# Filler products left out of the routing, and the last experts' combines issued one expert later

## The reference

```python
for layer in range(DEPTH):                       # DEPTH = 2
    hn = rms_norm(h, attn_norm_g[layer])
    mix = mixer_ab(...) if layer % 2 == 0 else mixer_c(...)
    h = h + mix
    h = h + hierarchical_moe(rms_norm(h, ffn_norm_g[layer]), ...)
return rms_norm(h, final_norm_g)

# hierarchical_moe: softmax over 4 groups, best group; top 2 of its 8 experts
# 32 experts in all; each: h = silu(xb @ w_gate[e]) * (xb @ w_up[e]);  y = h @ w_down[e]
# w_gate, w_up: 1024 x 512, w_down: 512 x 1024, all float32; y is added back with the gate's weight
```

## Time and profile before

| | |
|---|---|
| median of three runs | 1139.12 us |
| the profiled execution | 1137.95 us |
| its span, first to last instruction | 1136.1 us |
| mean granted clock of TensorE | 0.877 of full speed |
| TensorE matmul busy | 830.9 us (73%) |
| VectorE, ScalarE, GpSimd busy | 162.2, 153.8, 67.7 us |
| moved by DMA | 438.33 MB, mean 386 GB/s |
| chain that ended last | DMA 50%, PE 40%, issue 6% |

### The profile page before, as it was taken

The page is one execution under the profiler, slowest core; times in us unless marked ns, Lnnn a source line. Parts: engine busy times, 40 slices in busy tenths (PEclk is TensorE's granted clock), DMA queues, the critical chain, the costliest instruction groups (busy, mean ns, idle before and its releaser), DMA issues.

```text
span 1136.1 us, 13784 instructions
## 1 busy us (share of the span) xinstructions
PE 830.9 (73%) x5942; PEld 440.3 (39%) x5942; DVE 162.2 (14%) x438; ACT 153.8 (14%) x343; POOL 67.7 (6%) x88
## 2 busy tenths in 40 slices
PE   9999999835666474738789999955657464746876
PEld 7685684311313131314444576321313122211624
DVE  1143442000000000000014535100000000000002
ACT  2246231000000000000010444100000000000101
POOL 0010020000000000000001552000000000000000
PEclk9999999977878697868989999986878778877988
DMA  9942669999999999999999648999999999999994
GB/s 376 421 185 112 267 277 379 427 446 439 425 423 441 430 430 425 448 427 427 427 417 425 237 177 322 427 428 446 432 424 423 444 439 418 427 449 427 429 426 181
DMA packets 22544, 438.33 MB, mean 386 GB/s; under 512 B 2528, under 2 KB 3552, under 8 KB 7008
## 3 DMA queue, kind: packets, MB, share of 16 engines
q1 hardware_dynamic: 21232, 434.39, 90.2%
q10 hardware_dynamic: 1264, 3.23, 0.7%
HBM read 436.56 MB, written 1.05 MB: 385 GB/s over the span
## 4 chain that ended last, share of the span: by engine, by line
DMA 50%; PE 40%; issue 6%; DVE 2%; ACT 1%; POOL 1%; SPq 0%; POOLq 0%; DVEq 0%; ACTq 0%
DMA store<-in_w_gate 18%; DMA store<-in_w_down 18%; PE bank L1253 16%; DMA store<-in_w_up 14%; PE bank L954 5%; PE bank L996 5%; PE bank L1096 4%; PE bank L1393 1%; PE bank L933 1%; PE bank L1299 1%; PE bank L1197 1%; PE bank L1186 1%; PE bank L1320 0%; PE bank L962 0%; PE bank L1031 0%
## 5 line engine op out<-in xcount | busy, mean ns | idle before, releaser
L1253 PE MATMUL bank<-store,hg 128*32 128x512 f32 x2048 | 279.3, 701 | 217.8 <-DMA store<-in_w_up 113.4
L1253 PEld LDWEIGHTS bank<-store,hg 128*32 128x32 f32 x2048 | 72.0, 126 | 408.2 <-issue 258.2
L1253 PE MATMUL bank<-store 128*32 128x512 f32 x880 | 115.5, 676 | 62.0 <-DMA store<-in_w_down 60.6
L1253 PEld LDWEIGHTS bank<-store 128*32 128x32 f32 x880 | 33.3, 122 | 136.6 <-issue 134.8
L1772 DVE TENSOR_TENSOR store<-store,bank 128x512 f32<-128x512 f32 x16 | 11.0, 687 | 484.8 <-PE bank L1253 484.8
L954 PE MATMUL bank<-store,hg 128*128 128x512 f32 x160 | 71.2, 595 | 0.0
L1096 PE MATMUL bank<-store 128*128 128x256 f32 x256 | 64.6, 389 | 0.0
L996 PE MATMUL bank<-hg,store 128*128 128x256 f32 x256 | 58.2, 389 | 1.4 <-DMA store<-w_ab 1.4
L1186 PEld LDWEIGHTS bank<-store,hr 128*128 128x128 f32 x448 | 51.1, 192 | 12.6 <-issue 12.6
L642 POOL TENSOR_TENSOR store<-store,gate_all 128x256 f32<-128x256 f32 x16 | 9.8, 615 | 738.7 <-PE bank L933 720.8
L1186 PE MATMUL bank<-store,hr 128*128 128x128 f32 x448 | 53.7, 278 | 0.0
(11 more groups left out here) (210 smaller groups left out, 597.6 us busy)
## 6 DMA issues: line engine op xcount, KB each, us to landing
store<-in_w_up SPq DMA_DIRECT2D x12, 4096.0 KB, 25.6
store<-in_w_down SPq DMA_DIRECT2D x20, 2048.0 KB, 24.7
store<-in_w_up SPq DMA_DIRECT2D x16, 2048.0 KB, 16.5
store<-in_w_gate SPq DMA_DIRECT2D x16, 2048.0 KB, 12.2
store<-in_w_down SPq DMA_DIRECT2D x6, 4096.0 KB, 23.6
store<-in_w_down SPq DMA_DIRECT2D x14, 1024.0 KB, 27.8
store<-w_ab SPq DMA_DIRECT2D x6, 2048.0 KB, 31.5
store<-wo_ab SPq DMA_DIRECT2D x2, 2048.0 KB, 27.9
```

The source lines that it names most:

```text
L1253: op = pe.matmul(dst[rows, :], lhsT[:, q, rows], moving, start=(q == 0), stop=(q == steps - 1))
```

## The change

Two edits. The first removes `stay_warm` and its two calls: six products per layer, twelve in all, at L1119 and L1179. The second changes the last quad of each layer: odd experts use banks 6 and 7 instead of 4 and 5, the down products of expert e wait for the copies of expert e-2 instead of e-1 (so experts 0 and 1 wait for none), and each combine is issued behind the next expert's down products: down 0, down 1, combine 0, down 2, combine 1, down 3, combine 2, combine 3.

```diff
-                    act.activation(last_y[:, e, 1, :], bank[5][:, 0:P], ACT.Copy).then_inc(m["y_high"], 1)
+                    act.activation(last_y[:, e, 1, :], bank[5 + 2 * (e % 2)][:, 0:P], ACT.Copy).then_inc(m["y_high"], 1)
...
-            def stay_warm(dst, n):
-
-                for _ in range(n):
-                    pe.matmul(dst, ident, ones[:], start=False, stop=True, skip_group_check=True)
...
                             pe.wait_ge(once["second"], l + 1)
-                            stay_warm(bank[LOGIT_BANK][:, S:S + P], 3)
...
                 pe.wait_ge(hr_done, 4 * l + 2)
-                stay_warm(bank[5][:, 0:P], 3)
...
-                    else:
-                        pe.wait_ge(m["y_low"], last + e)
-                        pe.wait_ge(m["y_high"], last + e)
+                    if e >= 2:
+                        pe.wait_ge(m["y_low"], last + e - 1)
+                        pe.wait_ge(m["y_high"], last + e - 1)
...
-                                    op = pe.matmul(bank[4 + j][s * CAP:(s + 1) * CAP, 0:P], e_hT[:, q, e * CAP:(e + 1) * CAP],
+                                    op = pe.matmul(bank[4 + 2 * (e % 2) + j][s * CAP:(s + 1) * CAP, 0:P], e_hT[:, q, e * CAP:(e + 1) * CAP],
...
                             last_down(e, half)
-                            last_combine(e)
+                            if e:
+                                last_combine(e - 1)
+                        last_combine(QUAD - 1)
...
-                    dve.tensor_copy(last_y[:, e, 0, :], bank[4][:, 0:P]).then_inc(m["y_low"], 1)
+                    dve.tensor_copy(last_y[:, e, 0, :], bank[4 + 2 * (e % 2)][:, 0:P]).then_inc(m["y_low"], 1)
```

## The result

The changed kernel is slower by a little: 1141.0 us (median of 19 runs, 1138.02 to 1142.56) against 1138.49 us (19 runs of the kernel before beside them, 1136.85 to 1141.99). The ratio is 1.0016, 95% interval 1.0009 to 1.0023. The profiled execution took 1141.20 us, its span is 1139.3 us and its mean granted clock 0.867, where before had 1137.95, 1136.1 and 0.877. The median lies 1.0 us above the upper end of the forecast's range.

The account below looks back on a forecast made before the run. Waits run through expert weights (DMA 50%, TensorE 40% of the span), with both last quads on the path. Gains 0 + 0.70 + 0.40 = 1.1 us take the profiled 1137.95 to 1136.85; forecast median 1138.0, range 1136.3 to 1140.0.

Parts of the forecast that it names:

- Cost of the removal: 0, gain: 0: Routing: removing twelve filler products changes nothing, since the first gather waits for VectorE's pick anyway; 0 us.
- the rivals with a fall: Routing: TensorE's clock drops without fillers; once 1139.6 us (chance 0.07), in both layers 1141.2 us (0.05).
- The second term of the sum: Last quads: the new order gains 0.70 us in layer 0 and 0.40 in layer 1.
- The slow rival: Routing: without fillers TensorE idles and its clock drops to 1.2 GHz; chance 0.07 for once, 0.05 for twice.
- its twofold case: Routing of both layers: the clock falls in each, giving 1141.2 us; chance 0.05.
- The price of a fall: Routing: one clock fall costs 1.6 us, taken from half clock for 3 us at down 0 in layer 0.
- The changes of shape: Last quads: seven changes of product shape become five; an undisturbed train gains 0.69 us per layer.
- The block ends: Last quads: TensorE pauses for code every 256 instructions or so; ends forecast at 420 (layer 0), 271 and 527 (layer 1).
- No new wait in layer 0: Layer 0 last quad: the last half of weights lands at 588.3, before its use at 588.75.
- Trains of 13.3 and 13.3: Last quads: the train takes 13.3 us in each layer, from 14.02 and 13.67.
- The fast rival: Last quads: code blocks arrive in time, no pauses; gains 1.25 + 1.27 = 2.5 us, 1136.6 us; chance 0.12.
- the fetch takes all: Last quads: code fetch of 5.8 us per 256 instructions paces TensorE; gain -0.3 to +0.2, 1139.2 us; chance 0.10.

Follow-up runs that it names:

- e1: Kernel before with only the new order of the last quads, all fillers kept: 1138.74 us, ratio 1.0002 (0.9989 to 1.0014).
- e4: Kernel before with only the second filler set (ahead of the first gather) left out, old order: 1138.01 us, ratio 0.9990.
- e6: The changed kernel with the first filler set kept (new order, second set out): 1138.22 us, ratio 1.0000 to the kernel before.
- e8: Kernel before, all fillers and old order, with 18 instead of 24 unread products in the last quad, moving its code: 1138.60 us, ratio 0.9999.
- e10: Kernel before, old order, second fillers out, 20 unread products added ahead of the last quad's down products: 1141.51 us, ratio 1.0027.
- e9: New order, first fillers kept, second out, 20 unread products added ahead of the last quad's down products: 1142.34 us, ratio 1.0024 to the kernel before.
- e5: Kernel before, old order, both filler sets out, 30 instead of 24 unread products in the last quad, restoring code place: 1142.19 us, ratio 1.0044.
- e2: Kernel before with both filler sets out, old order kept: 1140.68 us, ratio 1.0019 (1.0007 to 1.0030).
- e3: Kernel before with only the first filler set (behind the wait for the second maximum) out, old order: 1138.50 us, ratio 0.9989.
- e12: Repeat of the kernel before with only the first filler set out, old order: 1138.36 us, ratio 0.9999 (0.9985 to 1.0012).

## Why the prediction was wrong

The step that failed is the first, "Cost of the removal: 0, gain: 0; what hides them is VectorE's chain and ScalarE's L737." It is right for the waits and wrong for the clock: the sum has no term for a clock that falls, and the rivals with a fall got only 0.07 (once) and 0.05 (twice). In its place the profiled execution showed 1.58 and 2.76 us lost in the two routings at a granted clock of 0.50, and the runs showed 1.0019 with the fillers out and the old order. The second term of the sum, 1.1 us for the order, did not show in the runs either (e1 1.0002). Point by point:

- *The removed products hide nothing on the path.* Right. The first gather came 4.31 us behind the mean-squares load, 0.06 behind the pick (168.78 + 0.43 to 169.27), as forecast. The profile now names ScalarE as the last of its waits.
- *The clock.* Wrong, and this decides. The slow rival had the mechanism and the place ("a clock of 0.50 between 168 and 172 or 698 and 702"; it was 169.9 and 698.97), and its twofold case gave 1141.2 us, where the profiled execution took 1141.20 and the median is 1141.0. That close a match is luck: the losses were larger (4.34 in the routings for my 3.2), and so were the gains (2.49 for 1.1). I gave it 0.05. The argument against it was that elsewhere the clock fell only behind idle pieces of 2.5 us and more. Here no idle piece between the mean squares and the gather was over 1.11 us (0.41, 1.09 and 0.91 in layer 0, 1.11 the longest in layer 1), and it fell all the same. The clock can fall behind several short ones with small products between them. And the argument was a misreading, for the trace of the kernel before has such a fall: in its final norm the clock falls at 1128.7, behind small products. From the end of the last combine on (1123.82) the weight loads stand idle 0.44 us at most, and then 0.67 in the piece in which the clock falls. In e1, e4, e6 and e8 it falls within the same few products. The kernel before (two rows of weight loads, then two stretches with the columns of the earlier trace rows):

```profile
1127.69 0.53 PEld L962 LDWEIGHTS bank<-ones,early 128*128 128x128 f32 x4
1128.89 0.93 PEld L947 LDWEIGHTS bank<-early,rstd 128*128 128x128 f32 x4 [0.67 <-POOL rstd L616]
...
1128.00:1129.00 1.00, 0.52 (x5) 0.33 (x3) 0.06 (x1) 0.23 (x1) 0.70 (x1) 0.84 0.00 0
1129.00:1130.00 1.00, 1.00 (x4) 0.82 (x4) 0.00 (x0) 0.00 (x0) 0.00 (x0) 0.50 0.00 0
```

- *The price of a fall.* I took 1.6 us, from down 0 in the earlier trace rows. It is 1.58 and 2.76 after, 1.3 to 3.6 over nine falls: it grows with how long the clock stays low (3.4 to 10.2 us), and 0.9 us more was lost before the last quad of layer 0, which I can't put down to one cause.
- *The changes of shape.* Right in kind. The gaps are 0.20 without the copy and 0.33, seven have become five. The gain of a train without pauses was forecast at 0.69 (11.67 to 10.98); e10 and e9 have 11.66 and 11.19, so 0.47. The last quads of all fourteen traces agree: the loads pause 0.20 us or more at every change of shape. The releaser in the row (VectorE's copy) is again no guide.
- *The block ends.* In layer 0 I placed one at 420 instructions, pause 0.55: it is behind load 59 of down 2, at 128 x 2 + 34 + 59 x 2 and some 6 waits = 414, and took 0.62. In layer 1 one at 271: load 3 of combine 0, about 267, with a pause of 1.24 where I had 1.5 (1113.9 to 1115.4). The one at 527 did not show. e5, which restores the code's place, pauses in combine 3 of layer 0 as before did, and so does e1 (1.49 and 1.54 us; before 0.46). In layer 0 the place goes with the code in these three; but in layer 1 before has two pauses and e5 none, so the code alone does not say whether a pause comes, and I can't derive its length. The Trainium skill, Runtime: NRT & Kernel Launch, section Instruction fetch mechanics, calls the crossing mostly hidden; pauses of 0.4 to 1.9 us without a releaser, in nine of the fourteen traces, speak against that for this dense train, if they are such crossings; the counts above say so, and no run settles it.
- *No new wait in layer 0.* Wrong by 0.66 us: down 2 stood 0.53 for its weights (0.33 without), the second half of down 3 0.46. The last half landed 31.3 us after its issue, not 28.8, and the train, which began warm, was ready for it earlier.
- *Trains of 13.3 and 13.3.* 12.50 and 12.68 after. Over the profiled executions the old order has a mean of 13.4 us (16 trains of eight kernels, e10 left out), the new one 13.2 (8 trains of four, e9 left out). The 1.1 us forecast for both layers shrinks to 0.4 in the mean. No pair of runs can tell that from nothing (e1 1.0002, e6 against e4, after against e2).
- *The fast rival, and "the fetch takes all".* The first did not happen. The second is near the truth in size, as the order's gain in the runs is near 0; that the fetch takes it is not shown.

The table of offsets closes the account of the profiled execution, which came out 3.25 us later than before where I had -1.1: +0.49 ahead of the first routing; +1.58 and +2.76 in the routings; +0.93 and -0.95 in the experts; -1.50 and -0.99 in the last quads (forecast -0.70 and -0.40); +0.01 between; +0.9 in the final norm. The last is the clock once more. It fell while twelve loads of the sums of squares ran (at 1129.05), where in the kernel before they were done when it fell (before, then after):

```profile
1126.36 1.41 PEld L1519 LDWEIGHTS bank<-ones,hr 128*128 128x128 f32 x12 [0.44 <-DVE hr L1923]
```

```profile
1128.67 2.32 PEld L1514 LDWEIGHTS bank<-ones,hr 128*128 128x128 f32 x12 [0.43 <-DVE hr L1918]
```

Left open: how often a fall comes in one execution of each kernel (only profiled executions show when the clock is low); why the four early falls all lie in kernels without the first set; what sets the length of a pause; e5 against e2. The lowest ratios are those of the old order with one set out, e3 at 0.9989 (0.9976 to 1.0001) and e4 at 0.9990 (0.9979 to 1.0000), and e12, which is e3 again, has 0.9999; I would not call that a gain.

## What to carry to other kernels

Filler products that no wait needs and no timeline shows on the path may still hold up the clock. Before they go, look at TensorE's idle pieces as a row and not each for itself, look through the whole trace for falls behind short idle pieces, and ask whether the work that follows releases the DMA stream. Leave out one set at a time; here no cost of either set alone could be measured, and both together cost 0.16 to 0.19% (0.44% in e5). A reorder that saves a few changes of shape of 0.2 to 0.3 us each is real in the trace and lost in the runs.

## What the runs showed of the hardware that I had not expected

- The clock fell to 1.2 GHz behind TensorE work broken by idle pieces of only 0.4 to 1.1 us (0.3 to 0.7 in the final norm of the kernel before), and a fall lasted from 3.4 us (after, layer 0) to 10.2 us (e2, layer 1).
- The same work met the fall at a different point in each execution, from 1.09 to 4.94 us behind the mean-squares load, or not at all. The Trainium skill, TensorE: Matmul & The Clock Gate, Part 1, says that the gate's own rhythm runs free and does not start with the kernel; the spread agrees.
- At the lower level 128 loads of 32 columns take 5.10 us (e1, layer 0, for most of the run) against 3.43, and the eight loads of a gather 1.78 against 0.97.
- One float32 product of 128 x 128 x 128 costs TensorE 0.23 us (4.56 / 20, granted clock 1.00) when many stand in a row.
